# The last feed-forward group and the final norm of a two-block model on one core: three token pieces (256, 128, 128) for two of 256, the norm weight multiplied in place by ScalarE, and the final scaling in wider products

## The reference

```python
def swiglu_ffn(x, w_in, w_down):
    a, b = jnp.split(x @ w_in, 2, axis=-1)
    return (jax.nn.silu(a) * b) @ w_down

def rmsnorm(x, g):
    xf = x.astype(jnp.float32)
    y = xf * lax.rsqrt(jnp.mean(xf * xf, axis=-1, keepdims=True) + EPS)
    return (y * g.astype(jnp.float32)).astype(x.dtype)
```

## Time and profile before

| What | Value |
|---|---|
| Median of three runs | 2463.27 us |
| The profiled execution's own time | 2463.75 us |
| Its span in the profile | 2461.4 us |
| Busy: PE, weight loads (PEld), DVE, ACT, POOL | 99%, 81%, 45%, 42%, 51% |
| Chain that ended last: PE, DVE, ACT | 89%, 6%, 3% |

### The profile page before, as it was taken

The page is one execution under the profiler, slowest core; times in us unless marked ns, Lnnn a source line. Parts: engine busy times, 40 slices in busy tenths (PEclk is TensorE's granted clock), DMA queues, the critical chain, the costliest instruction groups (busy, mean ns, idle before and its releaser), DMA issues.

```text
span 2461.4 us, 31870 instructions
## 1 busy us (share of the span) xinstructions
PE 2429.6 (99%) x12368; PEld 1987.1 (81%) x12368; DVE 1116.8 (45%) x2116; ACT 1030.3 (42%) x1544; POOL 1252.9 (51%) x1662
## 2 busy tenths in 40 slices
PE   8999999999999999999999999999999999999998
PEld 6877778888778787888888888878977788888887
DVE  7965765222795576422332113199266423211102
ACT  5344576323524467532443323243366533322321
POOL 5543554555553455455555554584443455555553
PEclk9999999999999999999999999999999999999999
DMA  4232122222222212222322222332221122222222
GB/s 157 90 107 79 61 76 71 95 95 102 88 93 74 86 52 86 70 102 94 112 95 95 96 101 86 130 119 70 94 70 69 69 103 94 94 95 94 99 98 86
DMA packets 64689, 224.30 MB, mean 91 GB/s; under 512 B 7399, under 2 KB 10983, under 8 KB 64412
## 3 DMA queue, kind: packets, MB, share of 16 engines
q1 hardware_dynamic: 62908, 216.49, 25.5%
q0 software_dynamic: 1632, 5.78, 0.8%
HBM read 219.57 MB, written 3.99 MB: 91 GB/s over the span
## 4 chain that ended last, share of the span: by engine, by line
PE 89%; DVE 6%; ACT 3%; POOL 1%; issue 1%; DMA 1%; SPq 0%; DVEq 0%; ACTq 0%
PE proj L186 78%; PE att L186 1%; PE proj L871 1%; PE att L850 1%; PE att L965 1%; PE att L951 1%; PE att L2146 1%; PE att L895 1%; PE att L906 1%; DVE h_low L537 1%; DVE hT L543 1%; POOL weight_low L163 1%; PE att L861 1%; DVE dq L1393 1%; ACT b_logits L2508 1%
## 5 line engine op out<-in xcount | busy, mean ns | idle before, releaser
L163 POOL TENSOR_TENSOR weight_low<-ring,weight_high 128x256 fp32r<-128x256 f32 x1584 | 1224.6, 805 | 1149.0 <-ACT weight_high L133 1126.0
L186 PE MATMUL proj<-h_high,weight_high 128*128 128x512 f32 x2000 | 787.5, 394 | 3.8 <-DVE h_low L537 1.5
L186 PE MATMUL proj<-h_high,weight_low 128*128 128x512 f32 x2000 | 778.8, 389 | 0.0
L186 PE MATMUL proj<-h_low,weight_high 128*128 128x512 f32 x2000 | 778.7, 389 | 0.0
L133 ACT ACTIVATE weight_high<-ring 128x1024 fp32r<-128x1024 f32 x391 | 411.9, 1054 | 400.8 <-PE proj L186 378.1
L186 PEld LDWEIGHTS proj<-h_high,weight_high 128*128 128x128 f32 x2000 | 375.5, 188 | 98.5 <-ACT sq_ L1006 5.3
L186 PEld LDWEIGHTS proj<-h_low,weight_high 128*128 128x128 f32 x2000 | 375.5, 188 | 79.0
L186 PEld LDWEIGHTS proj<-h_high,weight_low 128*128 128x128 f32 x2000 | 375.7, 188 | 75.1
L2744 DVE TENSOR_TENSOR b_big<-proj,b_big 128x512 f32<-128x512 f32 x42 | 29.0, 691 | 376.3 <-PE proj L186 376.3
L186 PE MATMUL proj<-b_act_high,weight_high 128*128 128x512 f32 (+1 forms) x352 | 134.9, 383 | 0.0
L186 PE MATMUL proj<-b_act_high,weight_low 128*128 128x512 f32 (+1 forms) x352 | 134.6, 382 | 0.0
(11 more groups left out here) (504 smaller groups left out, 3540.8 us busy)
## 6 DMA issues: line engine op xcount, KB each, us to landing
ring<-in_stream SPq DMA_DIRECT2D x396, 512.0 KB, 3.2
xT<-in_x SPq DMA_DIRECT2D x4, 512.0 KB, 6.8
idx<-gate_rows POOLq DMA_DIRECT2D x8, 256.0 KB, 4.0
out<-hT SPq DMA_DIRECT2D x8, 256.0 KB, 2.2
bias_rows<-bias_row SPq DMA_DIRECT2D x2, 512.0 KB
b_logits<-in_mem POOLq DMA_DIRECT2D x1, 1024.0 KB, 6.2
bias_rows<-bias_row SPq DMA_DIRECT2D x1, 768.0 KB
consts<-in_const SPq DMA_DIRECT2D x1, 576.0 KB, 10.0
```

The costliest lines, as they stand in the source:

```text
L163: self.s_low.on(pool.tensor_tensor(self.low[:, c % self.slots, cols], self.raw[:, c % self.slots, cols], self.high[:, c % HIGH, cols], ALU ...
L186: mm = pe.matmul(out, a, b, start=(k == 0 and i == 0), stop=(k == n - 1 and i == 2))
```

## The change

The last group is computed in three pieces: tokens 0 to 255 (`f2d7`), 256 to 383 (`f2_late`, into `att[0]`) and 384 to 511 (`f2_last`, into `att[1]`). The small products of the norm of a piece are issued before the k steps 8 and 13 of the next piece; those of the last piece come behind everything. ACT multiplies each tile of `xT` by its norm weight in place, behind the square of it, and DVE's scaling becomes a plain product of `xT` with the spread inverse root, over two tiles of 256 tokens or four tiles of 128 tokens with one instruction (512 values in each partition either way). DVE's order is written out in `endings`. SP issues four stores of two tiles for the first piece and two stores of four tiles for each of the others.

```diff
+ENDS = [(f"f2d{KD - 1}", (0, 1)), ("f2_late", (2,)), ("f2_last", (3,))]
...
-        return g if n == "f1" else g + [("ms_early", "a"), ("f2_late", OWN), ("ms_late", "a")]
+        ends = [("ms_end0", "a"), (ENDS[1][0], OWN), ("ms_end1", "a"), (ENDS[2][0], OWN), ("ms_end2", "a")]
+        return g if n == "f1" else g + ends
...
-    halves = [slice(0, HALF), slice(HALF, T)]
-    spread_bank = [att[5], att[3]]
+    ends = [slice(blocks[0] * P, (blocks[-1] + 1) * P) for _, blocks in ENDS]
+    spread_bank = [att[5], att[3], att[2]]
+    scales = [[(2 * i, 2 * i + 2) for i in range(4)], [(0, 4), (4, KD)], [(0, 4), (4, KD)]]
...
         def last_products(xs):
 
-            early, late = ([(xh[:, c], xl[:, c]) for xh, xl in xs] for c in halves)
-            product(f"f2d{KD - 1}", early)
-
-            def ready(k):
-                if k == 7:
-                    half_total(0)
-                if k == 13:
-                    half_spread(0)
-
-            W.product(pe, "f2_late", att[0][:, halves[1]], late, ready=ready)
+            parts = [[(xh[:, c], xl[:, c]) for xh, xl in xs] for c in ends]
+            product(ENDS[0][0], parts[0])
+            for i in (1, 2):
+
+                def ready(k):
+                    if k == 8:
+                        end_total(i - 1)
+                    if k == 13:
+                        end_spread(i - 1)
+
+                W.product(pe, ENDS[i][0], att[i - 1][:, ends[i]], parts[i], ready=ready)
...
         ffn("f2", "ffn2")
-        half_total(1)
-        half_spread(1)
+        end_total(2)
+        end_spread(2)
...
             if t < KD - 1:
                 S.s_sq.on(act.activation(square_place(S, "fin2", t), xT[:, t, :], ACT.Square))
+                s_weighed.on(act.activation(xT[:, t, :], xT[:, t, :], ACT.Copy, scale=vec("fin2", t)))
...
             S.s_sq.on(act.activation(hT[:, KD - 1, c], xT[:, KD - 1, c], ACT.Square))
+            s_weighed.on(act.activation(xT[:, KD - 1, c], xT[:, KD - 1, c], ACT.Copy, scale=vec("fin2", KD - 1)))
...
-        def half_scale(i):
-
-            G.moved(dve, ("ms_early", "ms_late")[i])
-            S.s_inverse.on(dve.reciprocal(S.norm_col[:, 2 * i:2 * i + 2], S.norm_col[:, 2 * i:2 * i + 2]))
+        def end_inverse(i):
+
+            b = slice(ENDS[i][1][0], ENDS[i][1][-1] + 1)
+            G.moved(dve, f"ms_end{i}")
+            S.s_inverse.on(dve.reciprocal(S.norm_col[:, b], S.norm_col[:, b]))
             dve.wait_ge(S.s_spread.sem, last + 1 + i)
-            for t in range(KD):
-                S.s_h.on(dve.scalar_tensor_tensor(hT[:, t, halves[i]], xT[:, t, halves[i]], vec("fin2", t),
-                                                  spread_bank[i][:, halves[i]], ALU.mult, ALU.mult))
+            dve.wait_ge(s_weighed.sem, KD + i)
+
+        def end_scale(i, at):
+
+            c, (t0, t1) = ends[i], scales[i][at]
+            wide = spread_bank[i][:, c].unsqueeze(1).to_broadcast([P, t1 - t0, c.stop - c.start])
+            S.s_h.on(dve.tensor_tensor(hT[:, t0:t1, c], xT[:, t0:t1, c], wide, ALU.mult))
+
+        def endings():
+
+            norm_sum(S, dve, "fin2", KD - 2)
+            end_add(0)
+            end_sum(0)
+            end_inverse(0)
+            end_scale(0, 0)
+            end_scale(0, 1)
+            end_add(1)
+            end_scale(0, 2)
+            end_sum(1)
+            end_scale(0, 3)
+            end_inverse(1)
+            end_scale(1, 0)
+            end_add(2)
+            end_scale(1, 1)
+            end_sum(2)
+            end_inverse(2)
+            end_scale(2, 0)
+            end_scale(2, 1)
...
-        for n, c in enumerate(halves):
-            for i in range(4):
-                sp.wait_ge(S.s_h.sem, KD * (last + n) + 2 * (i + 1))
-                s_out.on(sp.dma_start(out_dram[:, 2 * i:2 * i + 2, c], hT[:, 2 * i:2 * i + 2, c]), 16)
+        for n, c in enumerate(ends):
+            for i, (t0, t1) in enumerate(scales[n]):
+                sp.wait_ge(S.s_h.sem, scaled[n] + i + 1)
+                s_out.on(sp.dma_start(out_dram[:, t0:t1, c], hT[:, t0:t1, c]), 16)
```

More of the change, by code:

```diff
@@ L1783, in block_tile_of @@
         of[f"v{i}"] = "v_part0"
-    of["f2_late"] = f"f2d{KD - 1}"
+    for n, _ in ENDS[1:]:
+        of[n] = f"f2d{KD - 1}"
     return of
@@ L1941, in second_block @@
     s_late = sem("late_moved")
+    s_weighed = sem("s_weighed")
     s_lse, s_ln, s_dist, s_weight = (sem(n) for n in "lse ln dist weight".split())
@@ L2006, in ffn, with end_total, end_spread @@
                     power_rows()
-        def half_total(i):
-            out = G.open(pe, ("ms_early", "ms_late")[i])
+        def end_total(i):
+            out = G.open(pe, f"ms_end{i}")
             pe.wait_ge(S.s_sum.sem, last + 1 + i)
-            for b in (2 * i, 2 * i + 1):
+            for b in ENDS[i][1]:
                 mm = pe.matmul(out[:, b:b + 1], rstd[:, b * P:(b + 1) * P], S.ones[:, 0:1], start=True, stop=True)
             G.close(mm)
-        def half_spread(i):
+        def end_spread(i):
             pe.wait_ge(S.s_inverse.sem, last + 1 + i)
-            for b in (2 * i, 2 * i + 1):
+            for b in ENDS[i][1]:
                 mm = pe.matmul(spread_bank[i][:, b * P:(b + 1) * P], S.norm_col[:, b:b + 1].to_broadcast([P, P]), S.ident,
@@ L2652, in scalar @@
                 S.s_sq.on(act.activation(square_place(S, "fin2", t), xT[:, t, :], ACT.Square))
-        for i, name in enumerate(("ms_early", "ms_late")):
-            c = halves[i]
+                s_weighed.on(act.activation(xT[:, t, :], xT[:, t, :], ACT.Copy, scale=vec("fin2", t)))
+        for i, (name, blocks) in enumerate(ENDS):
+            c, b = ends[i], slice(blocks[0], blocks[-1] + 1)
             if i:
-                W.round(act, "f2_late")
-                act.wait_ge(s_late.sem, 1)
+                W.round(act, name)
+                act.wait_ge(s_late.sem, i)
             S.s_sq.on(act.activation(hT[:, KD - 1, c], xT[:, KD - 1, c], ACT.Square))
-            W.round(act, name)
-            bank = G.whole(act, name)
+            s_weighed.on(act.activation(xT[:, KD - 1, c], xT[:, KD - 1, c], ACT.Copy, scale=vec("fin2", KD - 1)))
+            W.round(act, f"ms_end{i}")
+            bank = G.whole(act, f"ms_end{i}")
             if i == 0:
                 act.wait_ge(S.s_h.sem, KD * last)
-            G.empty(act.activation(S.norm_col[:, 2 * i:2 * i + 2], bank[:, 2 * i:2 * i + 2], ACT.Sqrt, scale=1.0 / D,
-                                   bias=S.eps), name)
+            G.empty(act.activation(S.norm_col[:, b], bank[:, b], ACT.Sqrt, scale=1.0 / D, bias=S.eps), f"ms_end{i}")
     def vector(dve):
@@ L2772, in ffn, with end_add @@
                 norm_sum(S, dve, "mix", KD - 1)
-        def half_sum(i):
-            c, x = halves[i], xT[:, KD - 1, halves[i]]
+        def end_add(i):
+            name, x = ENDS[i][0], xT[:, KD - 1, ends[i]]
+            bank = G.whole(dve, name)
             if i == 0:
-                bank = G.whole(dve, f"f2d{KD - 1}")
-                G.empty(dve.scalar_tensor_tensor(x, bank[:, 0:HALF], 0.5, x, ALU.mult, ALU.add), f"f2d{KD - 1}")
-                norm_sum(S, dve, "fin2", KD - 2)
-            else:
-                G.whole(dve, "f2_late")
-                s_late.on(dve.scalar_tensor_tensor(x, att[0][:, c], 0.5, x, ALU.mult, ALU.add))
+                G.empty(dve.scalar_tensor_tensor(x, bank[:, ends[0]], 0.5, x, ALU.mult, ALU.add), name)
+            else:
+                s_late.on(dve.scalar_tensor_tensor(x, att[i - 1][:, ends[i]], 0.5, x, ALU.mult, ALU.add))
@@ L3110, in vector @@
         ffn("f2")
-        for i in range(2):
-            half_sum(i)
-            half_scale(i)
+        endings()
     def gpsimd(pool):
```

5 lines of the change are left out of this document (4 added, 1 removed).

## The result

The change took 2467.84 us, the median of 17 runs (2465.09 to 2470.65), against 2462.91 us for 17 runs of the kernel before (2460.74 to 2465.19): 4.9 us more, ratio 1.0022 with a 95% interval of 1.0015 to 1.0028. In a second comparison on another occasion (`e8_change_again`) it was 2466.51 against 2462.78 us, ratio 1.0015 [1.0006, 1.0024]. The change makes the kernel slower, by 4.9 us in the one comparison and 3.7 in the other. Executions of either kernel differ among themselves by some 5 us.

The account below looks back on a forecast made before the run. PE, busy 99% of the span, bounds the kernel, with a tail behind it. Last add 7.38 us later, less 2.37 us of tail, is +5.0 us on the median 2463.27: 2468.3 us, range 2464.8 to 2470.8 us.

Parts of the forecast that it names:

- the sum: Whole kernel: last add 7.38 us later, less 2.37 us saved in the tail, gives +5.0 us.
- The stream: PE's last 256 tokens: 132 matmuls of 128 tokens, bound by weight loads at 0.113 us each; last add 7.38 us later.
- this case: Weight loads bound PE's narrow matmuls, 0.107 to 0.120 us each; +4.2 to +5.9 us, up to +6.7; chance 0.77.
- Small products in the stream don't wait: PE's last pieces: sums for the norm's small products are ready before k = 8, so PE doesn't wait.
- The chain: Tail from the last add to the last scaling's end, 6.58 us before; add, total, spread and scaling get shorter.
- The scaling: DVE's last scaling: two wide instructions, 1.29 us in place of 3.22, saves 1.93 us.
- The square and sum: Tail, ACT then DVE: 0.90 us after against 0.91 before, as a scaling stands ahead of the sum; saves 0.
- The store: Last store, 2.62 us before: runs of 512 bytes, not 1 KB, add 0.15 us, bounds 0 and +0.8.
- ScalarE's copies at no cost: ACT's seven weight copies of 0.63 us each hide behind the squares; without cover up to 4.4 us in all.
- The quick load: Rival: PE's rounded weight loads are quicker and tokens still bind, 0.067 us each; -1.0 us; whole case's chance 0.12.
- the slow path of narrow products: Rival: PE's narrow rounded products fall to plain fp32's rate, two passes, 0.22 us each; +19 us, chance 0.07.
- The clock: Rival: PE's granted clock falls to 1.2 GHz inside the third piece; up to +12.5 us if loads slow too; chance 0.04.

Follow-up runs that it names:

- e8_change_again: The change run once more, unaltered, against the kernel before; 2466.51 against 2462.78 us, ratio 1.0015.
- The kernel of two halves: The change without its three pieces: two halves of 256 tokens, weight copies and wide products kept; 2463.35 us against 2462.20, ratio 1.0000.
- 384-and-128 kernel: The change with two pieces of 384 and 128 tokens in place of three; 2467.37 us, ratio 1.0019; run again 2466.66 us, ratio 1.0012.

## Why the prediction was right

The forecast was 2468.3 us for the median; it came out at 2467.84, and the loss was 4.9 us where the sum said 5.0. The mechanism was the forecast one, but that the numbers agree to 0.1 us is luck: the second comparison gave 3.7, and by the marks of one pair of profiles (+5.1) three errors, -0.13 in the stream, -0.12 in the chain and +0.30 in the store, cancel. The steps:

- *The stream*, 0.113 us for each narrow matmul by the loads of the one-column products: 0.1118 in the trace. The last add came 7.25 us later by the marks (23.88 - 16.63), where 7.38 was forecast. The cause is shown three ways: same distance with 224 tokens, shorter with fewer columns to load, and the stream back to 16.62 us without the pieces. Of its bounds, 0.120 and 0.107, neither was needed. (The range of this case by its own sum, +4.2 to +6.7 us, is 2467.5 to 2470.0, not 2467.3 to 2470.2.)
- *Small products in the stream don't wait*: right; PE is busy for 7.95 of the 8 us from 2451 to 2459.
- *The chain*: 2.52 us less up to the end of the last scaling were forecast, 2.64 came. The scaling is 1.29 us to the hundredth. The square and sum, put at 0, saved 0.10, since the DVE starts its sum 0.60 us after the scaling ahead of it.
- *The store*, +0.15 us taken out of 0 to 0.8: it was +0.45. This term was mis-sized. The reason given for it, shorter packets, is worth 0.12 to 0.15 us, as taken. The rest, 0.30, is a wait that the prediction didn't have: its wide scaling issues the second of the last stores 0.60 us after the first, which keeps the engines busy for 0.9. Before, they were issued 0.78 us apart and took 0.79 each. So the 1.93 us saved in the scaling are not all saved at the end of the span. The kernel of two halves, whose packets are as long as before's, has the same 3.07 us, by four stores 0.60 us apart.
- *ScalarE's copies at no cost*: right, by the stream of the kernel that has them without pieces and the 89.83 us ahead of the mark.
- *The other rivals.* The quick load and the slow path of narrow products are gone. The clock did not fall in the stream of the change's two profiles. But it did in a kernel with the same narrow matmuls, and the loads slowed down with it, so the rival's chance of 0.04 was low for the mechanism. Whether the change meets it in a part of its executions is open.

Two halves with the wide products are as fast as the kernel before, not faster; nothing tried beats it.

## What to carry to other kernels

When a product is split along the moving operand, every part pays its weight load again, and a load of 128 columns costs 0.11 us here: below some 235 tokens a matmul saves nothing (an estimate, where the line through 256 and 512 tokens meets the load; 224 tokens were measured at the load's 0.112, 256 at 0.120). Split down to the width at which the load is just hidden, and no further; where narrower results are needed, streaming up to that width costs nothing. A tail that waits for the last product is worth shortening only by less than the stream is lengthened, and behind the last compute look for what the stores still have to move, and whether a quicker scaling only puts them in a queue.

## What the runs showed of the hardware

- A load of a 128x128 rounded fp32 tile takes 0.112 us of PE when nothing hides it, 0.085 with 96 columns. With 64 columns and 128 tokens the distance is 0.060, where the tokens may bind as well. The Trainium skill's rule for a load ("TensorE: Matmul & The Clock Gate", LDWEIGHTS (loading the stationary operand)), columns over 1.2, gives 107, 80 and 53 ns; the trace lies 5 to 7 ns above each.
- Stores in runs of 512 bytes moved 289 GB/s at a full share of the DMA engines, stores in runs of 1 KB 333 GB/s.
- The granted clock fell to 0.50 inside an unbroken stream of matmuls, in both profiles of the 384-and-128 kernel: PE was busy for 1.70 of 1.70 us in the window in which it fell, and all it had done since its last matmul of 384 tokens, 3.5 and some 4 us earlier, was narrow matmuls and one-column products. The distance went from 0.11 to 0.21 us, with the loads.
